# In-place weight sums in two buffer sets, plain operands first, and down units between the products of the next pair

## What is computed

```
f = rmsnorm(h)                                   # D_MODEL = 1024
f = (silu(f @ w_gate) * (f @ w_up)) @ w_down     # D_FF = 2816
h = h + rmsnorm(f)
h = h + sigmoid(h @ w_ple_gate) * (p @ w_ple_proj)
```

## Time and profile before

| | |
|---|---|
| median of 3 runs | 2737.49 us (2736.22 to 2739.92) |
| profiled execution, own time | 2743.95 us |
| its span, first to last instruction | 2742.2 us |
| PE busy | 2656.9 us, 97% |
| DVE, ACT, POOL busy | 50%, 33%, 12% |
| mean granted TensorE clock | 0.99 |
| read from and written to HBM | 442 MB, 148 MB |

### The profile page before, as it was taken

The page is one execution under the profiler, slowest core; times in us unless marked ns, Lnnn a source line. Parts: engine busy times, 40 slices in busy tenths (PEclk is TensorE's granted clock), DMA queues, the critical chain, the costliest instruction groups (busy, mean ns, idle before and its releaser), DMA issues.

```text
span 2742.2 us, 39069 instructions
## 1 busy us (share of the span) xinstructions
PE 2656.9 (97%) x15096; PEld 2218.9 (81%) x15096; DVE 1366.9 (50%) x2279; ACT 905.7 (33%) x1746; POOL 317.1 (12%) x428
## 2 busy tenths in 40 slices
PE   6999999999999999999999999999999988999998
PEld 4777677777787779987777787777787978999998
DVE  5455552655565673134433566444224576445544
ACT  4345532443334443122222343333122433212122
POOL 0032000111000000001110001111000013233300
PEclk9999999999999999999999999999999999999999
DMA  7865587877777696655544576444445566665554
GB/s 252 315 226 183 197 291 252 270 250 248 235 248 262 226 352 193 224 182 177 177 156 161 206 266 238 168 159 157 158 164 186 193 264 229 215 210 205 185 204 142
DMA packets 226983, 591.40 MB, mean 216 GB/s; under 512 B 27232, under 2 KB 66016, under 8 KB 226400
## 3 DMA queue, kind: packets, MB, share of 16 engines
q1 hardware_dynamic: 226160, 586.80, 61.8%
q0 software_dynamic: 640, 2.10, 0.2%
HBM read 442.34 MB, written 147.65 MB: 215 GB/s over the span
## 4 chain that ended last, share of the span: by engine, by line
PE 85%; DVE 7%; DMA 3%; ACT 2%; issue 2%; SPq 1%; POOL 0%; DVEq 0%; ACTq 0%; POOLq 0%
PE ps L2353 48%; PE ps L2238 19%; PE ps L2268 9%; PE ps L2441 2%; PE ps L2461 1%; DMA wh<-whd 1%; PE ps L2523 1%; PE ps L2561 1%; PE ps L2545 1%; PE ps L2550 1%; DMA wld<-wl 1%; DVE wl L1770 1%; DMA og<-ogd 1%; DVE bl L1931 1%; DVE ssq L1881 1%
## 5 line engine op out<-in xcount | busy, mean ns | idle before, releaser
L2353 PE MATMUL ps<-bh,wh 128*128 128x512 f32 (+1 forms) x1008 | 366.7, 381 | 2.0 <-ACT ta L1383 1.3
L2353 PE MATMUL ps<-bl,wh 128*128 128x512 f32 (+1 forms) x1008 | 361.6, 376 | 0.0
L2353 PE MATMUL ps<-bh,wl 128*128 128x512 f32 (+1 forms) x1008 | 361.2, 375 | 0.0
L2353 PE MATMUL ps<-gh,wh 128*128 128x512 f32 (+1 forms) x880 | 289.8, 362 | 15.3 <-DVE mixF L1805 6.6
L2353 PE MATMUL ps<-gl,wh 128*128 128x512 f32 (+1 forms) x880 | 285.1, 357 | 0.0
L2353 PE MATMUL ps<-gh,wl 128*128 128x512 f32 (+1 forms) x880 | 284.8, 356 | 0.0
L1805 DVE TENSOR_TENSOR mixF<-mixF,ps 128x512 f32<-128x512 f32 (+1 forms) x160 | 112.1, 703 | 237.5 <-PE ps L2353 237.4
L2353 PEld LDWEIGHTS ps<-bh,wh 128*128 128x128 f32 x1008 | 184.6, 189 | 42.7 <-issue 7.0
L2353 PEld LDWEIGHTS ps<-bh,wl 128*128 128x128 f32 x1008 | 185.0, 189 | 36.0
L2353 PEld LDWEIGHTS ps<-bl,wh 128*128 128x128 f32 x1008 | 185.0, 189 | 33.4
L1770 DVE TENSOR_TENSOR wl<-w_raw,wh 128x1024 fp32r<-128x1024 f32 x102 | 125.3, 1229 | 151.9 <-ACT wh L1340 151.8
(11 more groups left out here) (245 smaller groups left out, 4599.6 us busy)
## 6 DMA issues: line engine op xcount, KB each, us to landing
wh<-whd SPq DMA_DIRECT2D x262, 512.0 KB, 3.6
wl<-wld SPq DMA_DIRECT2D x262, 512.0 KB, 4.6
w_raw<-in_w SPq DMA_DIRECT2D x102, 512.0 KB, 4.6
whd<-wh SPq DMA_DIRECT2D x102, 512.0 KB, 5.4
wld<-wl SPq DMA_DIRECT2D x102, 512.0 KB, 6.3
wh<-whd SPq DMA_DIRECT2D x66, 256.0 KB, 3.1
wl<-wld SPq DMA_DIRECT2D x66, 256.0 KB, 4.0
zt<-zd SPq DMA_DIRECT2D x16, 1024.0 KB, 7.6
```

The costliest lines, as they stand in the source:

```text
L2353: last = MM(out, ww[SLOT[n]][:, w_], xx[:, kk, r_], start=(j == 0 and x == 0), stop=(j == len(ks) - 1 and x == 2))
```

## The change

1. `S_X`, `S_W`: the order of the seven products. Before B11, T2, T3, T4, T1, B22, B21; after B11, B22, B21, T2, T3, T4, T1 with the weights A11, S4, A12, S2, S3, A22, S1. The evictions into xs0 to xs3 and the steps of swish and late are rewritten for it; ACT evicts two products of a pair in the place of one.
2. `weight_sums` writes its sums over the raw weights, and there are two sets of raw buffers (pairs of even and odd number). The buffers made1 to made4 are gone.
3. The raw weights of pair 0 are loaded in out 3 (part 1) and summed there (part 3), not in ple 2. Those of pair j > 1 are loaded at the last product of pair j-2.
4. The operand steps have new places: splits of B11, B22, B21 at parts 16 and 18 of ple 2, T1 and T2 at part 19, T4 and T3 and the other splits in ffn 3.
5. The four down units of the sets 0 to 3 stand behind products 1, 3, 4 and 5 of the first pair of the next set. Set 4's stand behind the whole last pair, which has buffers of its own (`gh_last`).
6. The norm P3's first squares wait for another split than the last.

```diff
-S_X = ["B11", "T2", "T3", "T4", "T1", "B22", "B21"]
-S_W = ["A11", "S2", "S3", "A22", "S1", "S4", "A12"]
-COMBOS = ["S1", "S2", "S3", "S4"]
+S_X = ["B11", "B22", "B21", "T2", "T3", "T4", "T1"]
+S_W = ["A11", "S4", "A12", "S2", "S3", "A22", "S1"]
+COMBOS = ["S1", "S3", "S2", "S4"]
+T_SUMS = ["T1", "T2", "T4", "T3"]
...
         for f in fs[::2]:
-            out += [("s", f, i) for i in range(len(S_X))]
-            if b and f == fs[0]:
-                down(b - 1)
-    down(len(FB) - 1)
-    return out
+            downs = down(b - 1) if b and f == fs[0] else []
+            for i in range(len(S_X)):
+                out.append(("s", f, i))
+                if i in (1, 3, 4, 5) and downs and b < len(FB) - 1:
+                    out.append(downs.pop(0))
+            out += downs
+    return out + down(len(FB) - 1)
...
-    beside("ple", 2, 2, "wraw", 0)
-    beside("ple", 2, 10, "wsum", 0, [0, 1])
-    beside("ple", 2, 17, "tsum", 0)
-    beside("ple", 2, 17, "xset", 0)
-    beside("ple", 2, 18, "tsum", 1)
-    beside("ple", 2, 18, "tsum", 2)
+    beside("out", 3, 1, "wraw", 0)
+    beside("out", 3, 3, "wsum", 0)
+    beside("ple", 2, 16, "xset", 0)
     beside("ple", 2, 18, "xset", 1)
-    beside("ple", 2, 18, "wsum", 0, [2, 3])
-    beside("ple", 2, 19, "tsum", 3)
-    beside("ple", 2, 19, "xset", 2)
-    for i, p in ((3, 1), (4, 3), (5, 5), (6, 7)):
-        beside("ffn", 3, p, "xset", i)
+    beside("ple", 2, 18, "xset", 2)
+    beside("ple", 2, 19, "tsum", 0)
+    beside("ple", 2, 19, "tsum", 1)
+    beside("ffn", 3, 1, "tsum", 2)
+    beside("ffn", 3, 1, "xset", 3)
+    beside("ffn", 3, 3, "tsum", 3)
+    beside("ffn", 3, 4, "xset", 4)
+    beside("ffn", 3, 6, "xset", 5)
+    beside("ffn", 3, 8, "xset", 6)
     for j in range(1, PAIRS):
-        first = 2 * (OF[GROUP[("s", 3, (2 * j - 2, 0))]] - FIRST[("ffn", 3)])
-        beside("ffn", 3, first, "wraw", j)
-        beside("ffn", 3, first, "wsum", j, [0, 1, 2, 3])
+        part = 2 * (OF[GROUP[("s", 3, (2 * j - 4, 6))]] - FIRST[("ffn", 3)]) if j > 1 else 0
+        beside("ffn", 3, part, "wraw", j)
+        beside("ffn", 3, part, "wsum", j)
...
+                    elif j == 1:
+                        sp.wait_ge(v_nm, (NORMS.index("F3") + 1) * KM)
+                        sp.wait_ge(gd, GROUP[("proj", 2, KM - 1)] + 1)
                     else:
-                        sp.wait_ge(w_sum, made_at(j - 1, 3))
+                        sp.wait_ge(w_lod, RAW_NO[made_unit(j - 2, "S1")] + 1)
...
+            def weight_sums(j):
+
+                gp.wait_ge(wr_in[j % 2], 64 * (j // 2 + 1))
+                TT(raw_part(j, "S1"), raw_part(j, "A21"), raw_part(j, "A22"), ALU.add).then_inc(w_sum, 1)
+                TT(raw_part(j, "S3"), raw_part(j, "A11"), raw_part(j, "A21"), ALU.subtract).then_inc(w_sum, 1)
+                gp.wait_ge(w_sum, made_at(j, "S1"))
+                TT(raw_part(j, "S2"), raw_part(j, "S1"), raw_part(j, "A11"), ALU.subtract).then_inc(w_sum, 1)
+                gp.wait_ge(w_sum, made_at(j, "S2"))
+                TT(raw_part(j, "S4"), raw_part(j, "A12"), raw_part(j, "S2"), ALU.subtract).then_inc(w_sum, 1)
...
+                    if m == (0, 0):
+                        act.wait_ge(v_pg, c * KM)
+                    elif m == (0, 1):
+                        act.wait_ge(y_out, 16 * KM * c)
...
-                    if f % 4 == 0 and f:
+                    if f == KF - 2:
+                        act.wait_ge(gd, last_operand_use(c))
+                    elif f % 4 == 0 and f:
                         act.wait_ge(gd, GROUP[("dn", c, KM - 1, f // 4 - 1)] + 1)
...
                         if name == "P3":
-                            act.wait_ge(w_lod, sum(SPLIT))
+                            act.wait_ge(w_lod, RAW_NO[made_unit(PAIRS - 2, "S1")] + 1)
```

More of the change, by code:

```diff
@@ L106, in down @@
     def down(b):
-        for i in range(KM * len(FB[b]) // 8):
-            out.append(("dn", b, i))
+        return [("dn", b, i) for i in range(KM * len(FB[b]) // 8)]
     for b, fs in enumerate(FB):
         for f in fs[::2]:
-            out += [("s", f, i) for i in range(len(S_X))]
-            if b and f == fs[0]:
-                down(b - 1)
-    down(len(FB) - 1)
-    return out
+            downs = down(b - 1) if b and f == fs[0] else []
[5 more added lines that the diff above has]
+    return out + down(len(FB) - 1)
 FFN_P = product_units()
@@ L226 @@
         _f, _i = _u.groups[0][0]
-        if _i in (5, 6):
-            SWISH[PART0[_n + 1]].append((_u.c, _f, 6 - _i, 0))
-            SWISH[PART0[_n + 1] + 1].append((_u.c, _f, 6 - _i, 1))
-        if _i == 6:
[L231 to L234, removed]
+        if _i == 2:
+            SWISH[PART0[_n + 1]].append((_u.c, _f, 0, "tanh"))
+            SWISH[PART0[_n + 1] + 1].append((_u.c, _f, 0, "gate"))
+        if _i == 5:
+            SWISH[PART0[_n + 1]].append((_u.c, _f, 0, "up"))
+        if _i == 6:
+            SWISH[PART0[_n + 1]].append((_u.c, _f, 1, "tanh"))
+            SWISH[PART0[_n + 1] + 1].append((_u.c, _f, 1, "gate"))
+            SWISH[PART0[_n + 1] + 1].append((_u.c, _f, 1, "up"))
+        if _i == 6:
+            LATE[PART0[_n + 1] + 2].append((_u.c, _f))
 RAW = [any(FIRST[ph] <= _n < BOUNDS[ph][1] for ph in (("z", 0), ("out", 0), ("ffn", 0), ("ple", 0)))
@@ L607, in build, with raw_part @@
         pjb3 = put("R", 0, "pjb3", [P, KM, WIDE])
[L609 to L618, removed]
+        raw_g.append(put("R", 2 * w_, "raw_g1", [P, 2, KM * P]))
+        raw_u.append(nc.alloc_sbuf_tensor_at("raw_u1", [P, 2, KM * P], f32, offset=sq_at))
+        def raw_part(j, what):
+            raw = raw_u[j % 2] if what in ("A21", "A22", "S1", "S3") else raw_g[j % 2]
+            return raw[:, :, 0:KM * P // 2] if what in ("A11", "A21", "S2", "S3") else raw[:, :, KM * P // 2:KM * P]
+        set_size = 4 * HW * 4
+        places = [("B", i * set_size) for i in range(7)] + [("C", i * set_size) for i in range(4)] \
+            + [("R", 2 * w_ + 2 * KM * P * 4 + i * set_size) for i in range(3)]
+        in_order = [(x, h) for x in ("B11", "B22", "B21", "T2", "T1", "T3", "T4") for h in range(2)]
+        place = dict(zip(in_order, places))
+        xh_ = [put(*place[(x, 0)], f"xh_{x}", [P, 4, HW], f32r) for x in S_X]
+        xl_ = [put(*place[(x, 1)], f"xl_{x}", [P, 4, HW], f32r) for x in S_X]
+        x_raw = {x: put(*place[(x, 1)], f"xraw_{x}", [P, 4, HW]) for x in T_SUMS}
+        xs = [put("R", 2 * w_ + 2 * KM * P * 4 + 3 * set_size, "xs0", [P, 2, HW])]
         xs += [nc.alloc_sbuf_tensor_at(f"xs{i}", [P, 2, HW], f32, offset=mixf_at + (i - 1) * 2 * HW * 4)
                for i in (1, 2, 3)]
+        gh_last, gl_last = [put("B", i * 2 * WIDE * 4, f"g_last{i}", [P, 2, WIDE], f32r) for i in range(2)]
         class Scratch:
@@ L1329, in split @@
                     f, i = UNITS[n].groups[0][0]
[L1330 to L1331 removed]
+                    act.wait_ge(w_sum, made_at(f // 2, S_W[i]))
                     act.wait_ge(gd, done(before))
[L1333 removed]
+                    A_(wh[s][:].rearrange("p (e n) -> p e n", e=2), raw_part(f // 2, S_W[i]), ACT.Copy
+                       ).then_inc(w_hi, 1)
                     return
@@ L1344, in evict @@
                 (m, _), g, c = u.groups[i], G0[n] + i, u.c
-                if u.kind in ("u",) or (u.kind == "dn" and m_block(u) > 0) or (u.kind == "s" and m[1]):
+                if u.kind in ("u",) or (u.kind == "dn" and m_block(u) > 0) or (u.kind == "s" and m[1] > 1):
                     return
@@ L2221, in operand @@
                 if u.kind == "dn":
+                    if wide(u.c) and u.groups[0][1][0][0] == KF - 2:
+                        return gh_last, gl_last
                     return (gh3, gl3) if wide(u.c) else (gh, gl)
```

134 lines of the change are left out of this document (64 added, 70 removed).

## The result

The changed kernel takes 2746.9 us (median of 8 runs, 2745.5 to 2754.2) against 2740.6 (8 runs, 2736.2 to 2744.5) on the same chip: a ratio of 1.0030, 95% interval 1.0018 to 1.0042. Forecast was 2720.8. The profiled execution is the longest of the eight, 2754.24 us around a span of 2752.4, so 7.4 us above the median: what the profile shows as lost can be some microseconds more than the median execution loses.

What follows compares the result with a forecast made beforehand. PE, busy 97% of the span, bounds the kernel, so only its gaps count: 5.0 + 9.7 + 3.4 - 1.4 = 16.7 us off the profiled 2743.95 gives 2727.2, as a median 2720.8; range 2711 to 2732.

Steps and rivals of the forecast that it cites:

- Ple 2, gain 5.0: Ple 2: moving POOL's first sums to out 3 frees DVE, closing 3.46 us of gaps and 1.7 us of low clock.
- the gap at the mean: Ple 2: PE's 2.03 us wait for norm F3's sum of squares, behind DVE operations lengthened beside POOL's sums; would close.
- the 1.23 us at the tanh: Ple 2: PE's wait at 2222 for the tanh that frees a bank, put down to delayed DVE; would close.
- Out 3, cost nothing: Out 3: added 2 MB of loads and four sums are covered; if short, one gap of a microsecond or two.
- The start of ffn 3, 16.7 to 7.0: Start of ffn 3: first two gaps close, the third grows to 5.1 us plus 1.4 low clock and 0.5; gain 9.7.
- the tight front of the rival: Rival, 0.23: ple 2 gives nothing back, or a late y store makes T3, S3, T4 and pair 1's sums slip; 2725.8 us.
- 5.1 between 0.1 and 6.1: Pair 1 of ffn 3, product 2: predicted gap in us for A12's load behind keep and raw weights, with its bounds.
- Down units, net gain 2.0: Down units: 3.4 us gained at the last full set, 1.4 lost at the first down units of sets 0 to 3.
- The 3.4 us at the end: Last full set's down units: the 2.3 us wait and the 1.1 us gap go.
- the far end of 9.1: Slowest landing, in us, allowed for the first down unit's load; 3.2 when clear, 6.5 behind raw weights.
- the slower one: Rival, 0.06: in each of nine pairs A12 or a down unit waits behind raw weights; 14 us slower, 2751.7.
- the lock of DVE and POOL: Rule used for ple 2 and out 3: two-SBUF-input DVE instructions and SBUF-reading GpSimd ones lock each other out; 4.3 us in ple 2.

Runs made afterwards that it cites:

- experiment 5: The changed kernel with the first pair's four weight sums moved back from out 3 to ple 2: ratio 1.0046 to the kernel before.
- experiment 2: The changed kernel with POOL's sums of pair 2 and on waiting for the third product of the pair ahead: ratio 0.9973 to the kernel before.
- experiment 3: The changed kernel, raw weights from pair 2 on asked for at the second product of pair j-1, not the last of j-2: 0.9930, 2720.8 us.
- the first experiment: The changed kernel with POOL's weight sums on 8 of 512 columns, every instruction, wait and transfer kept: ratio 0.9972 to the kernel before.
- experiment 6: The changed kernel, raw weights at the second product of pair j-1 and a set's first down unit behind the third product: ratio 0.9929.
- experiments 9 and 10: The changed kernel, raw weights at pair j-1's fourth product with down units, first without; first down unit behind third product (9: 0.9921) or second (10: 0.9928).

## Why the prediction was wrong

The sum up to the second pair came out as predicted, in part by other steps.

- *Ple 2, gain 5.0.* Both gaps closed, no idle time, no low clock; undone in experiment 5 it costs 4.4 us. Right, and by the mechanism given for the gap at the mean; for the 1.23 us at the tanh it is not shown.
- *Out 3, cost nothing.* One gap of 1.25 us appeared, at 2159.08, of the size that the text allowed for. The weights that end it were asked for right behind the 2 MB of raw weights and landed after 12.3 us, where the same load took 8.6 before. It is there in all thirteen kernels with these loads in out 3 (0.64 to 1.69 us), with the sums and, in experiment 5, without. A small miss. From the start of out 3 to the first product the two executions differ by 114.99 - 110.96 = 4.0 us, 5.0 having been predicted.
- *The start of ffn 3, 16.7 to 7.0.* 14 products take 44.99 us without a gap. Before they took 2255.16 to 2317.4, a loss of 17.2; after, 2248.90 to 2301.4, a loss of 7.5. The gain is the 9.7 predicted, but by luck, since the gap stood elsewhere: the tight front of the rival (xl_T, 4.6 us) came first, by POOL's sums and not by the store of y, and hid the load of A12 (0.86). Without the sums that load's gap is 6.0, where I had taken 5.1 between 0.1 and 6.1.
- *Down units, net gain 2.0.* The 3.4 us at the end came. The first down unit of the sets did not cost 1.0 each but 2.2 (8.7 in four), since the load took 7.7 to 8.7 us to land and not 6.5, and a low clock followed three of the four gaps. Both my rows and the far end of 9.1 were there; I took a value near the good end. With the clock they are worth 6 to 11 us by experiments 2 and 3, of which the prediction had 4.
- *The step that failed: "The raw weights come a pair earlier, so POOL's sums are never near their due time after pair 1".* It is true of the sums' own due time, and I priced the move at nothing for it. The question was not when the sums are needed but what runs beside them. Before, each sum waited until the previous pair's weight of the same kind had been split (the w_lod waits of weight_sums), and that held the whole block of about 11 us back to the middle of a pair (2399.83 above), where DVE mostly evicts from PSUM; the second set of buffers took these waits away, and the same block now starts when the raw weights land. In the pair behind the down units that is the chain from the last product through swish and split to the low part of S2. 11.7 us of waits and the clock: 15.6 us by experiment 2.

The two together are the 27 us by which experiment 3 is faster than the changed kernel, and the forecast missed by 26. None of the rivals was this: the slower one had as its price the raw weights in front of A12 or of a down unit, 4.6 us in each of nine pairs; they cost 0.9 us at A12 of pair 1, 8.7 at four down units and nothing in the rest. I had used the lock of DVE and POOL for ple 2 and for out 3, and did not carry it to the pairs, where it mattered four times over. The low clock behind new gaps was priced only where a gap was foreseen. Two sums are off by 0.1 us, which changes nothing: 13.84 + 2.8 is 16.6, and the first down units of the sets 0 to 3 waited 3.8 - 1.1 = 2.7 us before.

Still open is why some gaps of 2 us were followed by a low clock and others were not: from the third pair on the first experiment keeps four waits of 1.7 to 2.4 us at down units and shows one such stretch; the changed kernel has eight waits of 1.8 to 3.1 us there and seven stretches. Open, too, is what delays the load of the first down unit in the experiments 6 and 9.

## What to carry to other kernels

A wait that paces an engine off the critical path may be what keeps it out of the critical engine's way: when buffers are doubled and the wait goes, ask at which moment the freed work will now run and what stands beside it then. Where DVE and POOL both read SBUF, give POOL's block a place by an explicit wait; here one wait was worth 15.6 us. Keep a bulk transfer away from the load that follows it (here 2 MB issued 4 us ahead took it from 4.5 to 8 us; 2 MB issued 0.5 us behind a load did little or nothing), and price each new gap with the clock that may follow.

## What was not expected of the hardware

- Only some DVE instructions lengthen beside POOL's sums. Those with both inputs in SBUF went from 0.76 to 2.9 us (128x576) and from 1.35 to 3.6 (128x1152). One with an input in PSUM (xs<-xs,ps) took 0.74 us in the middle of the sums, at 2270.59. The Trainium skill, page "SBUF — State Buffer", section "Who interferes with whom", says just this: a DVE instruction with at most one SBUF input, outside the 2-port perf modes, does not contend with GpSimd, and one with two does when GpSimd reads SBUF. The runs agree; the rule was at hand and was not applied to the pairs.
- A load of 1 MB landed in 7.7 to 8.7 us when issued 4 us behind 2 MB of raw weights, in 4.5 to 4.6 with an eighth of their bytes or with them 5 us behind, and in 4.4 to 4.6 with all of them 0.5 us behind (experiments 9 and 10). The page that the prediction cites (the Trainium skill, page "DMA: Bandwidth & Descriptors", section "Queues, rings and completion order") says that each DMA engine takes the descriptors of a queue in ring order. The runs agree for the raw weights: they delay a load behind them and, in the experiments 9 and 10, not one ahead. The 6.6 to 8.1 us of experiment 6 have the raw weights behind them, and what delays those loads was not measured by itself.
- Nearly all columns taken out of POOL's sums and a single wait in front of them gave the same time (0.9972 and 0.9973).
